# One block of a two-block network on one core: another interleaving of the state-space branch with its projections

## The chip, the cores and the metric

One core of a Trainium2 chip runs the whole program. The metric is the device time of one execution in microseconds (us), the median of several runs.

## The reference, cut to what matters

The network has two blocks. The first mixes tokens in two branches (a neighbourhood attention, "na", and a bidirectional state-space branch, "SSD") and then runs a mixture of 16 experts; the second block is a transformer of two layers. The change lies in the SSD branch and at its seam with the attention. There are 512 tokens and 256 context tokens, 4 groups of 8 heads of 64, chunks of 128 tokens (4 chunks, and 2 of context) and a state of 128. All of it is float32.

```python
xbc = silu(dwconv(h @ w_in[xBC], conv_w, conv_b))        # width 5, along the tokens
xs, Bm, Cm = split(xbc)
dt = softplus(dt_raw + dt_bias); a = dt * A; a_cs = cumsum(a) in a chunk
states = einsum(Bc, exp(a_cs[-1] - a_cs), x)              # one per chunk and direction
h = decay * h + states                                    # scan over the chunks
y_diag = (C B^T * exp(a_cs[l] - a_cs[s])) @ x             # inside a chunk
y_off  = (C @ h_prev) * exp(a_cs)
y = y_f + y_b + d_skip * xs
u = y * silu(z); u = u * rsqrt(mean(u*u over a group) + eps) * g   # z = h @ w_in[z]
```

## The kernel before, in words

Each engine has a program of its own, written as Python generators; a step ends at `yield`. Semaphores order the engines. `weave(main, filler, per)` and `pace(main, filler, plan)` merge two generators on each engine: `weave` puts one filler step in whenever `per` has added up to 1, `pace` puts plan[i] filler steps ahead of main step i. So PE, ScalarE (act), VectorE (dve) and GpSimd (pool) each execute the merged order strictly.

**Main: `pe_chunks(g)` and its fellows**, 15 steps a group. Five *state steps*, here S0 to S4: in each, VectorE or GpSimd weighs x by decay (`weigh`, L1028), PE makes two state products (L1039), VectorE adds them to the carried state (L1206 to L1215). In S0 to S3 the previous group's output is scaled to unit mean square (`dve_scale_z`, `pool_scale_z`, after `act_rstd`), turned by PE (`pe_finish`) and stored (`act_finish`). Then ten *chunk steps*, C0 to C9; n counts half chunks of four heads. ScalarE makes the exponents of half chunk n+1 (eight one-head passes, L1124, from rows that `load_rows` fetches by DMA, L1104) and the exponential of half chunk n (L1133); VectorE selects (L1252); GpSimd multiplies by C B^T (L1306, the matrix M of a half chunk); two steps later PE multiplies M by x (`pe_second`, L1072) and at odd n adds the products with the states (L1079). GpSimd and VectorE sum the parts (L1268, L1316 to L1320, L1277), VectorE multiplies by silu(z) (L1280), and ScalarE squares the result (`act_second`, L1167).

**Filler: `pe_proj(g+1)`**, 8 steps. Four convolution steps of x: PE products (L720, 10.5 us a step), two ScalarE copies into a padded row (L730, L733), five VectorE passes (L754, L758), two ScalarE silus (L739, L742), and PE turns the result of the step before (`pe_turn_x`). Then four z steps: one tile of z's products (L295, 7 us) and a silu by ScalarE (L956). `proj(0)` runs ahead of group 0, woven with `pe_dt` (the step sizes dt and their sums).

With per = 0.56 the filler steps of group g+1 fall behind the main steps S1, S3, C0, C2, C3, C5, C7 and C9: two convolutions in the state steps, two in the chunk steps, z in the rest. Beside group 3 run the attention's q and k products (`pe_na_qk` 0 and 1, L1531 and L1724, eight steps, the last two after the last main step). After that the attention (`pe_att_2`) has V's products (`pe_na_v`) as filler, by `PLAN1`; V reads a reordered copy of the input (`HTn`), made by `act_by_blocks` and `dve_by_blocks` in the room of B and C once `PHASE_C` (all of the SSD branch stored) is reached.

PSUM has 8 banks. Main takes from `PA` (five), the filler from `PG` (three), each time the bank that was taken longest ago, after a wait until it is free.

Of the kernel before, what the change touches and what calls it, by code (L numbers as in the profile page):

```python
# [157 lines left out]
def pace(main, filler, plan):  # L158

    for n in plan:  # L160
        for _ in range(n):
            next(filler, None)
        next(main, None)
    for rest in (main, filler):
        for _ in rest:
            pass

# [11 lines left out]
def build(nc, A, out):  # L179
    ctx = ExitStack()  # L180
    with ctx:
# [66 lines left out]
        PALL, PA, PG = list(range(8)), [3, 4, 5, 6, 7], [0, 1, 2]  # L248
        rings = [PS]
# [476 lines left out]
        def act_conv(act, nm, i, ti, dx, dc, before):  # L726
# [7 lines left out]
                *up(S("act_pad"), ("free", (nm, i, 2)), ("pad", (nm, i))))  # L734
            act.wait_ge(*at("acc", (nm, i)))
# [196 lines left out]
        def act_turn_x(act, g, i):  # L932
            key = ("tx", g, i, 4)
            act.wait_ge(*at("full", key))
            act.activation(xs2[g % 2][:, 4:6, i * 128:(i + 1) * 128], r3(PS.of(key)[:, 0:256], 128), ACT.Copy, bias=0.0, scale=1.0).then_inc(  # L935
                *up(S("act_xs"), ("free", key), ("xs", g, i, 4)))

        def act_proj(act, g):
            for i in range(4):
# [4 lines left out]
                act_conv(act, ("x", g), i, 4 * g + i, xsF[i % 2][:, 0:512], xsF[i % 2][:, 512:768], before)  # L944
                if g > 1 and i == 1:
                    act.wait_ge(*at("gone", g - 2, "pool"))
                    act.wait_ge(*at("gone", g - 2, "pe"))
                if i:
                    act_turn_x(act, g, i - 1)
# [81 lines left out]
        def pe_chunks(pe, g, pool):  # L1031
            xsT, BT = xs2[g % 2], BT2[g % 2]
            for m, (d, n, c) in enumerate(SWEEP):
# [6 lines left out]
                if d:  # L1040
                    if n in (2, 3) and g:
                        pe_finish(pe, g - 1, n - 2, pool)
# [67 lines left out]
        def act_exponents(act, g, n):  # L1110
# [7 lines left out]
            for d in range(2):  # L1118
# [16 lines left out]
        def act_chunks(act, g):  # L1135
            for d in range(2):
                load_rows(act, g, 0, d)
            for n in range(5):
                if n == 0 and g:
                    act_rstd(act, ("ssd", g - 1), ssy, 4)  # L1140
                if n in (2, 3) and g:
                    act_finish(act, g - 1, n - 2)
# [12 lines left out]
            if g == 3:  # L1155
                yield from idle(2)
                act_rstd(act, ("ssd", g), ssy, 4)
# [12 lines left out]
        def act_finish(act, g, part):  # L1170
            for i in (2 * part, 2 * part + 1):
# [5 lines left out]
                act.wait_ge(*now(S("act_fin")))  # L1177
                act.dma_start(yD[:, t, :], yTb[t % 2]).then_inc(*up(S(f"y_out{t % 2}"), ("yD", t), by=16))

        def dve_scale_z(dve, g):  # L1180
            zs = zs2[g % 2]
            dve.wait_ge(*at("uu", g, 3))
            dve_rstd(dve, ("ssd", g), ssy, 4, mean=512.0)
            dve.wait_ge(*at("rstd", ("ssd", g)))
            for c in (0, 2):
                dve.tensor_scalar(zs[:, c, :], zs[:, c, :], ssy[:, c:c + 1], None, ALU.mult).then_inc(*up(S("dve_zn"), ("zn", g, c)))

        def pool_scale_z(pool, g):
            zs = zs2[g % 2]
            pool.wait_ge(*at("rstd", ("ssd", g)))  # L1190
            for c in (1, 3):
                pool.tensor_scalar(zs[:, c, :], zs[:, c, :], ssy[:, c:c + 1], None, ALU.mult).then_inc(*up(S("pool_zn"), ("zn", g, c)))

        def dve_chunks(dve, g):
            for m in range(3):
                weigh(dve, 0, g, m)
            for m, (d, n, c) in enumerate(SWEEP):
# [18 lines left out]
                if d:  # L1216
                    if n == 0 and g:
# [10 lines left out]
            mark(("gone", g, "dve"), S("dve_y"))  # L1228
            if g == 3:
                yield from idle(2)  # L1230
                dve_scale_z(dve, g)

# [21 lines left out]
        def dve_second(dve, g, n):  # L1254
            c, hq = divmod(n, 2)
            if hq == 0:
                return
            for d in range(2):
# [3 lines left out]
                if c or g:  # L1262
                    pg, pc = (g, c - 1) if c else (g - 1, 3)
                    dve.wait_ge(*at("u", pg, pc) if d == 0 else at("ty1", pg, pc))
# [3 lines left out]
                dve.tensor_tensor(r3(TY[d], 64), r3(PS.of(key), 64), ev_, ALU.mult).then_inc(*up(S("dve_y"), ("free", key), ("ty", g, c, d)))  # L1268

        def dve_join(dve, g, n):  # L1270
# [5 lines left out]
            dve.wait_ge(*at("yd", g, c, 1))  # L1276
            dve.tensor_tensor(TY[0], PS.of(("y", g, c)), TY[0], ALU.add).then_inc(*up(S("dve_y"), ("free", ("y", g, c))))  # L1277
            dve.wait_ge(*now(S("dve_y")))
            dve.wait_ge(*at("zs", g, c))
            dve.tensor_tensor(zs[:, c, :], zs[:, c, :], TY[0], ALU.mult).then_inc(*up(S("dve_y"), ("u", g, c)))  # L1280

        def pool_chunks(pool, g):
            for m in range(3):
                weigh(pool, 1, g, m)
            for m, (d, n, c) in enumerate(SWEEP):
                weigh(pool, 1, g, m + 3)
                if d:
                    if n == 0 and g:
# [9 lines left out]
            if g == 3:  # L1298
                yield from idle(2)
                pool_scale_z(pool, g)  # L1300

# [6 lines left out]
        def pool_second(pool, g, n):  # L1308
# [419 lines left out]
        def act_by_blocks(act):  # L1728

            for kt in range(1, 8, 2):  # L1730
# [3 lines left out]
        def dve_by_blocks(dve):  # L1734
            for kt in range(0, 8, 2):
# [28 lines left out]
        def act_na_qk(act, n):  # L1764
            if n == 0:
                wait_all(act, SET0)
                act.dma_start(dcon, dsrc).then_inc(*up(S("dcon_in"), ("dcon",), by=16))
# [9 lines left out]
        def act_na_v(act, m):  # L1777
            for i in range(6):
# [26 lines left out]
        def dve_na_v(dve, m):  # L1805
            for i in range(6):
# [81 lines left out]
        PLAN1 = [0, 2, 1, 1, 1, 1] + [1, 1, 1, 1, 2] + [1, 1, 1, 1, 0] + [1, 0, 1, 1, 0, 1] + [1, 1, 1, 1, 0] + [1, 2, 1, 2, 1, 2, 1, 2, 2, 2]  # L1888
# [839 lines left out]
        def chain(*parts):  # L2728
            for part in parts:
                yield from part  # L2730

# [203 lines left out]

        def sp_program(sp):
# [4 lines left out]
            for g in range(3):  # L2941
                weave(idle(15), sp_proj(sp, g + 1), 0.56)
# [190 lines left out]
```

## Time and profile before

| | us |
|---|---|
| median of 3 runs | 4037.88 (4037.07 to 4039.29) |
| the profiled execution, its own time | 4034.85 |
| its span, first to last instruction | 4032.9 |
| SSD groups 0 to 3, first state product to last product with the states | 303.9 to 765.7 |
| granted TensorE clock, mean of the span | 0.967 |

PE is busy for 91% of the span, VectorE 28%, ScalarE 19%, GpSimd 11%. A row of the timeline gives start, duration, engine, line, operation and count, and in brackets the idle time before it with what released it. A float32 matmul of 512 columns shows as two records. ACTq is ScalarE's DMA issue.

### The profile page before, as it was taken

To read this page: it belongs to the slowest core of one execution; us is meant where nothing else is said; L and a number is where in the kernel's file an instruction comes from. 1 tells how busy PE (TensorE), PEld (TensorE's weight loads), DVE (VectorE), ACT (ScalarE), POOL (GpSimd) and SP (SyncE) were. 2 spreads that over 40 slices of the span, in tenths; PEclk is the share of its full clock that TensorE was granted. 3 is DMA by queue.
4 is the path that set the end of the run, shared out by engine and by line. 5 is a ranking of instruction groups with operands and counts; after the bars stand their busy time and mean duration, and the time that the engine had idled before them with its cause. 6 is when DMAs were issued, how large, how long until landed. Compare 5 with 4: busy or idle time off the path is not lost.

```text
span 4032.9 us, 32976 instructions
## 1 busy us (share of the span) xinstructions
PE 3663.4 (91%) x12600; PEld 1762.2 (44%) x12600; DVE 1137.1 (28%) x2594; ACT 782.8 (19%) x1786; POOL 450.8 (11%) x405
## 2 busy tenths in 40 slices
PE   6898888899999888888888888899999999999999
PEld 3354444444444443333233334555444445554444
DVE  2335444434310220311101114443221134432211
ACT  2024344322310210000000003332110123221100
POOL 1001223412100000000000002100221011012210
PEclk8899898999999989999999998999999999999999
DMA  7322223211212569999999992102222120022220
GB/s 253 125 75 75 79 63 94 87 37 50 79 63 88 189 250 409 409 409 409 409 409 409 409 398 73 37 27 84 83 72 80 51 90 32 28 97 69 84 71 34
DMA packets 302153, 634.08 MB, mean 157 GB/s; under 512 B 32499, under 2 KB 145763, under 8 KB 301743
## 3 DMA queue, kind: packets, MB, share of 16 engines
q1 hardware_dynamic: 240480, 591.96, 39.1%
q10 hardware_dynamic: 61519, 40.02, 3.5%
q8 instruction: 102, 1.67, 0.2%
q14 instruction: 52, 0.43, 0.0%
HBM read 625.50 MB, written 10.24 MB: 158 GB/s over the span
## 4 chain that ended last, share of the span: by engine, by line
PE 53%; DMA 18%; DVE 3%; SPq 1%; ACT 1%; issue 1%; POOL 0%; DVEq 0%; ACTq 0%
PE psum L295 26%; DMA arena<-in_w_exp_up_dram 7%; DMA arena<-in_w_exp_gate_dram 7%; PE psum L1531 6%; DMA arena<-in_w_exp_down_dram 4%; PE psum L2799 4%; PE psum L2763 4%; PE psum L2304 4%; PE psum L1359 2%; PE psum L1387 1%; PE psum L2784 1%; PE psum L2253 1%; PE psum L1368 1%; SPq L264 1%; PE psum L2694 1%
## 5 line engine op out<-in xcount | busy, mean ns | idle before, releaser
L295 PE MATMUL psum<-arena 128*128 128x512 f32 (+1 forms) x3200 | 1309.8, 568 | 17.1 <-ACT arena L935 11.9
L295 PEld LDWEIGHTS psum<-arena 128*128 128x128 f32 x3200 | 612.4, 193 | 699.2 <-issue 660.3
L2304 PE MATMUL psum<-arena 128*64 128x512 f32 x3072 | 696.5, 598 | 148.8 <-DMA arena<-in_w_exp_up_dram 76.2
L2304 PEld LDWEIGHTS psum<-arena 128*64 128x64 f32 x3072 | 234.4, 137 | 592.1 <-issue 571.6
L1531 PE MATMUL psum<-arena 128*128 128x512 f32 x768 | 352.8, 614 | 0.0
L720 PE MATMUL psum<-arena 128*128 128x512 f32 (+1 forms) x768 | 274.5, 517 | 1.3 <-ACT arena L538 1.3
L1531 PEld LDWEIGHTS psum<-arena 128*128 128x128 f32 x768 | 147.5, 196 | 193.2 <-issue 192.4
L1465 DVE CUSTOM_DVE_ANT_0 arena<-psum,arena 128x512 f32<-128x512 f32 (+3 forms) x224 | 114.0, 546 | 384.5 <-PE psum L1359 376.3
L2842 POOL TENSOR_SCALAR arena<-arena 128x512 f32<-128x512 f32 x88 | 138.6, 1576 | 696.2 <-ACT arena L2821 696.2
L720 PEld LDWEIGHTS psum<-arena 128*128 128x128 f32 x768 | 152.5, 201 | 125.4 <-issue 114.7
L2848 DVE SCALAR_TENSOR_TENSOR arena<-arena 128x512 f32<-128x512 f32 x88 | 66.2, 752 | 426.6 <-POOL arena L2842 426.6
L1407 ACT ACTIVATE arena<-arena 128x512 f32<-128x512 f32 (+3 forms) x224 | 134.3, 601 | 134.3 <-DVE arena L1465 133.7
L2369 DVE TENSOR_TENSOR arena<-arena,psum 128x512 f32<-128x512 f32 x32 | 22.0, 689 | 462.0 <-PE psum L2304 462.0
L2799 PE MATMUL psum<-arena 128*128 128x512 f32 x352 | 152.0, 592 | 0.0
L2763 PE MATMUL psum<-arena 128*128 128x512 f32 x352 | 151.7, 592 | 0.0
L2821 ACT ACTIVATE arena<-psum 128x512 f32<-128x512 f32 x88 | 52.5, 597 | 509.7 <-PE psum L295 478.2
L1368 PE MATMUL psum<-arena 128*128 128x128 f32 x576 | 85.7, 277 | 55.9 <-DVE arena L1472 30.7
L1542 POOL TENSOR_TENSOR arena<-arena 128x512 f32<-128x512 f32 x48 | 61.3, 1277 | 608.3 <-ACT arena L1538 595.2
L307 PE MATMUL psum<-arena 128*128 128x128 f32 (+3 forms) x442 | 67.6, 300 | 53.4 <-ACT arena L730 18.9
L1368 PEld LDWEIGHTS psum<-arena 128*128 128x128 f32 x576 | 68.4, 142 | 107.6 <-DVE arena L1472 38.1
L2763 PEld LDWEIGHTS psum<-arena 128*128 128x128 f32 x352 | 66.6, 189 | 84.7 <-issue 84.7
L2206 POOL TENSOR_TENSOR arena<-arena 128x128 f32<-128x128 f32 x32 | 12.9, 433 | 809.1 <-PE psum L307 593.2
(276 smaller groups left out, 3022.9 us busy)
## 6 DMA issues: line engine op xcount, KB each, us to landing
arena<-in_w_exp_gate_dram SPq DMA_DIRECT2D x128, 1024.0 KB, 18.6
arena<-in_w_exp_up_dram SPq DMA_DIRECT2D x128, 1024.0 KB, 18.6
arena<-in_w_exp_down_dram SPq DMA_DIRECT2D x128, 1024.0 KB, 18.8
arena<-in_w_in_dram SPq DMA_DIRECT2D x64, 1024.0 KB, 5.3
arena<-in_w_up_dram SPq DMA_DIRECT2D x88, 512.0 KB, 4.8
arena<-in_w_ada_dram SPq DMA_DIRECT2D x24, 1024.0 KB, 7.9
arena<-in_w_down_dram SPq DMA_DIRECT2D x20, 1024.0 KB, 4.9
arena<-acs_scratch ACTq DMA_DIRECT2D x64, 256.0 KB, 4.5
```

The lines of the kernel that those rows point to most:

```text
L295: mm = pe.matmul(shaped(b, l, r), l, r, start=kt == 0, stop=kt == nkt - 1)
L307: t = pe.transpose(b[0:m, c * k:(c + 1) * k], x, ident[0:k, 0:k])
L720: mm = pe.matmul(b[:, 0:z - a], wt(nm, kt, 512)[:, i * 128:(i + 1) * 128], HT[:, kt, a:z], start=kt == 0, stop=kt == 7)
L1359: pe.matmul(b[:, 0:u.nk], J.queries(u, a, z), J.keys(u, a, z), start=True, stop=True).then_inc(*up(S("pe_score"), ("full", ("s2", J.id, i, ...
L1368: t = pe.transpose(b[:, 128 * j:128 * j + 128], J.score(i, c)[:, 128 * j:128 * j + 128], ident)
L1407: act.activation(J.score(i, c), J.score(i, c), ACT.Exp, bias=sv2(i, c)[:, 0:1], scale=-1.0, accum_out=sv2(i, c)[:, 1:2]).then_inc(*up(S("a ...
L1465: dve.tensor_tensor_reduce(out=J.score(i, c), in0=PS.of(("s2", J.id, i, c))[:, 0:u.nk], in1=J.table(u, c), scale=-J.scale(u), scalar=3.0e3 ...
L1531: mm = pe.matmul(b, wt(nm, kt, 256)[:, i * 128:(i + 1) * 128], src[:, kt, 0:512], start=kt == 0, stop=kt == 7)
L2304: mm = pe.matmul(banks[n][64 * j:64 * j + 64, :], lhs[:, kt, 64 * j:64 * j + 64], w, start=kt == 0, stop=kt == 2 * nkb - 1)
L2763: mm = pe.matmul(banks[i], actT[:, kt, i * 128:(i + 1) * 128], wt(nm, kt, 512), start=kt == 0, stop=kt == 21)
L2799: mm = pe.matmul(b, actT[:, kt, i * 128:(i + 1) * 128], wt(nm, kt, 512), start=kt == 0, stop=kt == 21)
L2842: pool.tensor_scalar(accs3[n % 4], pads3[n % 4][:, 0:512], w3(L, 0, ti_of(s, i)), None, ALU.mult).then_inc(*up(S("pool_acc"), ("acc3", L, n)))
```

## The change

It does seven things.

1. `pace` with `PLAN0` takes the place of the weaves. Each group now has z tiles 1 to 3 of its own group ahead of S0, S1 and S2; the four convolution steps of the next group ahead of C0, C2, C4 and C6; z tile 0 of the next group ahead of C8. So `proj(0)` runs only five steps ahead of group 0, woven with `dt`.
2. The eight q and k steps run ahead of C0, C1, C2, C4, C5, C6, C8, C9 of group 3, and V's first two tiles ahead of its last two (idle) steps. V's `HTn` copies now wait for the last product of group 3 alone. `PLAN1` gives no V tile between the first two attention steps.
3. Banks: main `PA1` = 4 to 7, filler `PG1` = 0 to 3.
4. The product inside a chunk is added to the state part at once by VectorE (`dve_second`), and GpSimd's two additions come in another order.
5. The scale of a group's output: ScalarE computes rsqrt straight from the sums (`act_z_guess`, one table set), in S1; VectorE scales three tiles and GpSimd one, in S2; the turns come in S3 and S4.
6. `load_rows` for n+1 is issued after all eight exponent passes of n, not after the first four.
7. `act_turn_x` stands between the pad copies and the silu. The load of `dcon` is issued earlier.

```diff
         PALL, PA, PG = list(range(8)), [3, 4, 5, 6, 7], [0, 1, 2]
+        PA1, PG1 = [4, 5, 6, 7], [0, 1, 2, 3]
...
-                if d == 0:
-                    for e in range(2):
-                        load_rows(act, g, n + 1, e)
+            for d in range(2):
+                load_rows(act, g, n + 1, d)
...
-                if n == 0 and g:
-                    act_rstd(act, ("ssd", g - 1), ssy, 4)
-                if n in (2, 3) and g:
-                    act_finish(act, g - 1, n - 2)
+                if n == 1 and g:
+                    act_z_guess(act, g - 1)
+                if n in (3, 4) and g:
+                    act_finish(act, g - 1, n - 3)
...
+        def act_z_guess(act, g):
+            act.preload_act_table_set(LNEXP)
+            act.wait_ge(*now(S("act_uu")))
+            act.wait_ge(*at("eps"))
+            act.activation(small[:, 0:4], ssy, ACT.Ln, bias=eps, scale=1.0 / 512).then_inc(*up(S("act_rs")))
+            act.wait_ge(*now(S("act_rs")))
+            act.activation(small[:, 0:4], small[:, 0:4], ACT.Exp, bias=0.0, scale=-0.5).then_inc(*up(S("act_rs"), ("rs", ("ssd", g))))
...
+            dve.wait_ge(*now(S("dve_y"), 1))
+            dve.tensor_tensor(TY[0], PS.of(("y", g, c)), TY[0], ALU.add).then_inc(*up(S("dve_y"), ("free", ("y", g, c)), ("tyy", g, c)))
...
-            pool.tensor_tensor(TY[0], TY[0], TY[1], ALU.add).then_inc(*up(S("pool_ty"), ("ty1", g, c)))
             pool.wait_ge(*now(S("pool_ty")))
-            pool.tensor_tensor(TY[0], TY[0], TY[2], ALU.add).then_inc(*up(S("pool_ty"), ("ty3", g, c)))
+            pool.tensor_tensor(TY[1], TY[1], TY[2], ALU.add).then_inc(*up(S("pool_ty")))
+            pool.wait_ge(*at("tyy", g, c))
+            pool.wait_ge(*now(S("pool_ty")))
+            pool.tensor_tensor(TY[0], TY[0], TY[1], ALU.add).then_inc(*up(S("pool_ty"), ("ty3", g, c)))
...
         def act_by_blocks(act):
+            act.wait_ge(*at("gone", 3, "pe"))
...
         def dve_na_v(dve, m):
+            if m == 0:
+                dve_na_rope(dve, 1, 3)
+                dve_by_blocks(dve)
+                dve.wait_ge(*at("gone", 3, "pool"))
...
-        PLAN1 = [0, 2, 1, 1, 1, 1] + [1, 1, 1, 1, 2] + [1, 1, 1, 1, 0] + [1, 0, 1, 1, 0, 1] + [1, 1, 1, 1, 0] + [1, 2, 1, 2, 1, 2, 1, 2, 2, 2]
+        PLAN1 = [0, 0, 1, 1, 1, 1] + [1, 1, 1, 1, 2] + [1, 1, 1, 1, 0] + [1, 0, 1, 1, 0, 1] + [1, 1, 1, 1, 0] + [1, 2, 1, 2, 1, 2, 1, 2, 2, 2]
...
+        PLAN0 = (([1, 1, 1, 0, 0] + [1, 0] * 5) * 3 + [1, 1, 1, 0, 0] + [1, 1, 1, 0, 1, 1, 1, 0, 1, 1] + [1, 1])
...
-            weave(pe_proj(pe, 0, PALL), pe_dt(pe), 0.5)
-            for g in range(3):
-                weave(pe_chunks(pe, g, PA), pe_proj(pe, g + 1, PG), 0.56)
-            main = pe_chunks(pe, 3, PA)
-            for _ in range(3):
-                next(main)
-            weave(main, chain(pe_na_qk(pe, 0, PG), pe_na_qk(pe, 1, PG)), 0.57)
+            banks = PALL[:]
+            proj = pe_proj(pe, 0, banks)
+            weave(take(proj, 5), pe_dt(pe), 0.5)
+            banks[:] = PG1
+            filler = chain(proj, *[pe_proj(pe, g, PG1) for g in (1, 2, 3)], pe_na_qk(pe, 0, PG1), pe_na_qk(pe, 1, PG1), pe_na_v(pe, 0, PG))
+            pace(chain(*[pe_chunks(pe, g, PA1) for g in range(4)]), filler, PLAN0, False)
```

The other engines' programs change in the same way.

## Rows read from the trace of the kernel before

**Rows 1.** Busy time by stretch: groups 1, 2, 3, then to the attention's first turn.

```profile
422.80:460.40 37.60, 33.62 (x107) 18.74 (x106) 19.83 (x32) 10.58 (x16) 6.99 (x5) 0.95 0.25 83
460.40:549.60 89.20, 75.67 (x241) 42.06 (x240) 41.62 (x65) 47.75 (x107) 27.35 (x22) 0.89 0.24 72
549.60:678.90 129.30, 111.61 (x347) 61.90 (x346) 61.80 (x97) 58.42 (x123) 34.33 (x27) 0.89 0.25 73
678.90:765.70 86.80, 77.79 (x254) 42.55 (x253) 49.34 (x96) 36.91 (x95) 37.73 (x29) 0.94 0.38 113
765.70:823.20 57.50, 47.91 (x136) 24.95 (x136) 17.46 (x44) 14.30 (x27) 13.93 (x19) 0.91 0.18 54
```

**Rows 2.** PE's waits, 270 to 800 us: total, times, longest.

```profile
PE psum L307 <- ACT arena L730: 18.9, 6, 5.7
PE psum L1072 <- POOL arena L1306: 12.1, 8, 2.8
PE psum L295 <- ACT arena L935: 11.9, 3, 4.0
```

**Rows 3.** Timeline of PE in group 1.

```profile
460.66 10.49 PE L720 MATMUL psum<-arena 128*128 128x512 f32 x32
...
512.38 1.94 PE L1079 MATMUL psum<-arena 128*128 128x512 f32 x4
514.16 7.04 PE L295 MATMUL psum<-arena 128*128 128x512 f32 x16
...
537.21 1.97 PE L1072 MATMUL psum<-arena 128*128 128x64 f32 x8 [2.76 <-POOL arena L1306]
538.97 3.73 PE L1079 MATMUL psum<-arena 128*128 128x512 f32 x4
```

**Rows 4.** Timeline of ScalarE in C0 to C3 of group 1.

```profile
483.43 0.49 ACT L742 ACTIVATE arena<-arena 128x256 f32<-128x256 f32 x1
...
485.39 0.93 ACTq L1104 DMA_DIRECT2D arena<-acs_scratch  x2
...
487.65 1.28 ACT L1133 ACT_TABLE_LOAD   x1
488.95 0.63 ACT L1133 ACTIVATE arena<-arena 128x512 f32<-128x512 f32 x1
489.48 1.26 ACT L1124 ACTIVATE arena<-arena 128x128 f32<-128x128 f32 x4
...
493.93 0.36 ACT L733 ACTIVATE arena<-psum 128x256 f32<-128x256 f32 x1
...
500.31 0.72 ACT L739 ACTIVATE arena<-arena 128x512 f32<-128x512 f32 x1 [4.71 <-DVE arena L758]
```

**Rows 5.** Timeline of VectorE in the same group, the convolution's four later passes.

```profile
460.05 4.20 DVE L758 SCALAR_TENSOR_TENSOR arena<-arena 128x772 f32<-128x772 f32 x4
...
495.42 4.86 DVE L758 SCALAR_TENSOR_TENSOR arena<-arena 128x772 f32<-128x772 f32 x4
```

**Rows 6.** Timeline of GpSimd in the same group, the last two matrices M.

```profile
531.10 1.27 POOL L1306 TENSOR_TENSOR arena<-arena 128x512 f32<-128x512 f32 x1 [7.90 <-ACT arena L1133]
...
535.89 1.27 POOL L1306 TENSOR_TENSOR arena<-arena 128x512 f32<-128x512 f32 x1
```

**Rows 7.** Timeline of PE ahead of group 0: z tiles 0 and 1, then dt's sums.

```profile
271.38 13.93 PE L295 MATMUL psum<-arena 128*128 128x512 f32 x32
...
286.36 0.57 PE L829 MATMUL psum<-arena 128*128 128x192 f32 x2 [0.40 <-DVE arena L882]
```

**Rows 8.** Timeline of all engines at the seam to the attention.

```profile
784.00 3.65 PE L307 MATMUL psum<-arena 128*128 128x128 f32 x16 [8.00 <-POOL arena L1192]
...
787.94 0.69 ACT L1176 ACTIVATE arena<-psum,arena 128x512 f32<-128x512 f32 x1 [0.97 <-DMA yT_scratch<-arena]
...
799.25 0.46 ACTq L1676 DMA_DIRECT2D arena<-rpb_copies  x1
...
807.49 0.69 DVE L1465 CUSTOM_DVE_ANT_0 arena<-psum,arena 128x512 f32<-128x512 f32 x1 [7.54 <-POOL arena L1694]
```

More of the change, by code:

```diff
@@ L155, in weave, with pace @@
         pass
-def pace(main, filler, plan):
+def pace(main, filler, plan, empty=True):
     for n in plan:
@@ L163, in pace, with chain, take @@
         next(main, None)
-    for rest in (main, filler):
+    for rest in (main, filler) if empty else (main,):
         for _ in rest:
             pass
+def chain(*parts):
+    for part in parts:
+        yield from part
+def take(steps, n):
+    for _ in range(n):
+        next(steps)
+        yield
 def run(steps):
@@ L724, in pe_conv, with act_conv @@
                 mm.then_inc(*up(S("pe_conv"), *keys))
-        def act_conv(act, nm, i, ti, dx, dc, before):
+        def act_conv(act, nm, i, ti, dx, dc, before, between=None):
             pad, prev = pads1.take((nm, i))
@@ L734, in act_conv @@
                 *up(S("act_pad"), ("free", (nm, i, 2)), ("pad", (nm, i))))
+            if between:
+                between()
             act.wait_ge(*at("acc", (nm, i)))
@@ L933, in act_turn_x @@
             key = ("tx", g, i, 4)
+            if g > 1 and i == 0:
+                act.wait_ge(*at("gone", g - 2, "pool"))
+                act.wait_ge(*at("gone", g - 2, "pe"))
             act.wait_ge(*at("full", key))
@@ L943, in act_proj @@
                     before = [("full", ("BF", 3, 2))]
[L944 to L949, printed above, removed]
+                act_conv(act, ("x", g), i, 4 * g + i, xsF[i % 2][:, 0:512], xsF[i % 2][:, 512:768], before,
+                         (lambda: act_turn_x(act, g, i - 1)) if i else None)
                 yield
@@ L1227, in dve_chunks @@
                 yield
-            mark(("gone", g, "dve"), S("dve_y"))
+            mark(("gone", g, "dve"), S("dve_u"))
             if g == 3:
-                yield from idle(2)
+                yield
                 dve_scale_z(dve, g)
+                yield
         def dve_first(dve, g, n):
@@ L1298, in pool_chunks @@
             if g == 3:
-                yield from idle(2)
+                yield
                 pool_scale_z(pool, g)
+                yield
         def pool_first(pool, g, n):
@@ L1734, in dve_by_blocks @@
         def dve_by_blocks(dve):
+            dve.wait_ge(*at("gone", 3, "pe"))
             for kt in range(0, 8, 2):
@@ L1777, in act_na_v @@
         def act_na_v(act, m):
+            if m == 0:
+                act_by_blocks(act)
+                act.wait_ge(*at("gone", 3, "pool"))
             for i in range(6):
@@ L2997, in act_program @@
             weave(act_bc(act), act_ada_rest(act), 1)
-            weave(act_proj(act, 0), act_dt(act), 0.5)
-            for g in range(3):
-                weave(act_chunks(act, g), act_proj(act, g + 1), 0.56)
-            main = act_chunks(act, 3)
-            for _ in range(3):
-                next(main)
-            weave(main, chain(act_na_qk(act, 0), act_na_qk(act, 1)), 0.57)
+            proj = act_proj(act, 0)
+            weave(take(proj, 5), act_dt(act), 0.5)
+            filler = chain(proj, *[act_proj(act, g) for g in (1, 2, 3)], act_na_qk(act, 0), act_na_qk(act, 1), act_na_v(act, 0))
+            pace(chain(*[act_chunks(act, g) for g in range(4)]), filler, PLAN0, False)
             wait_all(act, PHASE_C)
-            act_by_blocks(act)
             act.wait_ge(*at("rpb"))
@@ L3067, in pool_program @@
             pool_start(pool)
-            run(idle(8))
-            for g in range(3):
-                run(pool_chunks(pool, g))
-            main = pool_chunks(pool, 3)
-            for _ in range(3):
-                next(main)
-            weave(main, chain(pool_na_qk(pool, 0), pool_na_qk(pool, 1)), 0.57)
+            filler = chain(idle(27), pool_na_qk(pool, 0), pool_na_qk(pool, 1), idle(6))
+            pace(chain(*[pool_chunks(pool, g) for g in range(4)]), filler, PLAN0, False)
             pool_near_zero(pool)
@@ L3077, in pool_program @@
             pool_near_mid(pool, 0)
-            pace(pool_att_2(pool, NEAR), chain(idle(12), pool_na_qk(pool, 2), pool_na_qk(pool, 3), idle(20)), PLAN1)
+            pace(pool_att_2(pool, NEAR), chain(filler, idle(6), pool_na_qk(pool, 2), pool_na_qk(pool, 3), idle(20)), PLAN1)
             pool_branch_na(pool)
```

67 lines of the change are left out of this document (32 added, 35 removed).

## The prediction, as it was put on record

> **What bounds the kernel now.** I read the page first, then busy time by stretch, PE's waits, and the timelines of PE, ScalarE, VectorE and GpSimd. Everything behind the attention's start is work that the diff leaves alone, so it moves as a block; what counts is when PE gets there. Groups 1 and 2 take 126.8 and 129.3 us [rows 1]. PE's work in a group at full clock is 97.2: four convolution steps at 10.3 and four z tiles at 6.9 from start to start [rows 3], 8.6 of state products, 7.0 of M's products, 6.9 with the states, 5.9 of turns and small ones. So some 30 us a group are waits or slow clock. The waits end on a padded copy (18.9 us over the branch), on M (12.1) and on a turned copy (11.9) [rows 2]; the granted clock is 0.89 in the chunk steps [rows 1]. After a wait of only 2.8 us the eight M records and four state records take 5.5 us, where the latter four alone take 3.7 against 1.9 [rows 3]: half speed, 1.2 GHz for 2.4.
>
> What the reader should see next is whose chain the waits end. ScalarE is busy for 47.8 of 89.2 us in the chunk steps [rows 1], yet between two convolution silus it never rests: it works, issues DMAs, or waits for the five VectorE passes between padded copy and silu, in order. From one silu's end (483.8) to the next (501.3) are 17.5 us [rows 4], against 14.7 of PE's work in such a pair of steps (10.3 convolution, 0.65 turn, 3.7 products).
>
> **The change, part by part.**
>
> *Banks four and four.* The waits on L730 and L935 are for one of the filler's three banks: a convolution takes two, its turns two more. With four they go, 30.8 us in all [rows 2]. What is late next is the chain behind M.
>
> *Four convolutions beside the chunks.* Now each pair C(2j), C(2j+1) holds one on ScalarE. The loop from silu end to silu end, from [rows 4]: eight exponent passes 2.5; issue of rows 0.95; table load and exponential 1.8; then a wait, since the rows are asked for only after all eight passes: 4.1 from issue to use (485.39 to 489.48), of which 2.8 are filled, so 1.3; eight passes 2.5; issue 0.95; exponential 0.55; the square 0.75, and 0.3 of wait, as GpSimd needs 4.8 us between two M [rows 6]; padded copies 0.85; VectorE's five passes 0.65 + 4.2 [rows 5]; silus 1.05. That is 18.4, and PE's 14.7 is hidden under it. It holds three times a group, once without the square (17.4).
>
> The chunk steps then take: first convolution 10.3, padded copy 0.45, VectorE 4.85, silus 1.05, that is 16.7 to the first silu's end; 17.4 + 18.4 + 18.4 to the fourth, 70.9; from there passes 2.5, table and exponential 1.8, M 1.3, and the last M 4.8 + 1.3 after it [rows 6]: 82.6. PE has then waited some 5 us (M of the last half chunk is all that is left behind z tile 0) and does its last products at half speed, 5.5 us as in [rows 3]. Sum 88.1, where the chunk steps now take 89.2 [rows 1]. PE's work there is only 65.6, so 22 us stay idle or slow: at C2 and C3 6 us, at C5 and C7 up to 4 each, at C8/C9 8.
>
> *z beside the states.* Three z tiles 20.7, states 8.6, turns 2.4: 31.7 of work. New waits: x's last turn now stands right ahead of the first state product, which needs VectorE's copy and weighing (1.4 us of passes, 1.8 taken). In S3 the output's turns wait for the scaling: VectorE, after the state additions of S2 (1.9 behind PE), does five small operations (1.0) and three tiles, not two (2.0): less PE's 1.7 of products, 3.4. Behind it the states' additions are queued and two banks of main's four come late, 0.7; slow clock 1.4. Sum 39.0, now 37.6 in group 1. The shorter rsqrt chain (one table set for two) costs and gives nothing: it lies beside S1 and S2.
>
> A group thus takes 39.0 + 88.1 + 0.3 = 127.4 against 126.8 and 129.3, mean 128.05. For the three groups with convolutions, group 0 taken like the others: -2.
>
> *Ahead of group 0.* The sums over dt wait for a product that VectorE ends at 286.3. Now z tiles 0 and 1 cover that, and 0.40 remain [rows 7]. With tile 0 alone PE is through at 278.35: a wait of 8.0, less the 0.4. The sums and the turn behind it lose 1.4 in slow clock and in a copy that tiles 2 and 3 covered. Sum +9.
>
> *Group 3.* Now 86.8 [rows 1] with six q and k tiles. Without a convolution ScalarE's loop is 6.7 a half chunk (2.5 + 4.2 of rows), PE's 10.6: PE bound, chunk steps 83.6 of work and 1.4 slow. Two of the eight tiles (20.7) and z tiles 1 to 3 (20.7) with a turn (0.65) are work done earlier or later than now, so 39.0 + 85.0 - 42.0 = 82.0; I keep 1 for small waits: 83 for 86.8, -4.
>
> *The seam.* Now a wait of 8.0 for the scaling, at 776.0 [rows 8]. The new order puts V's first tiles there. They need the reordered input; on VectorE that stands behind the last chunk's sums (4.2 us after PE's last product), the last rope (2.4) and four copies (1.4): 8.0. So one wait of 8 takes the place of another. Then come the two tiles (14), which hide the scaling, and the turns. Behind the turns everything of the attention's first softmax is serial: ScalarE stores four tiles, each pair waiting for the store two before (787.94, issued 2.1 earlier), so storing ends 7.9 after the turns begin; tables are asked for at 8.3; from there to the first reduction is 8.2 (799.25 to 807.49) [rows 8]; four reductions, two exponentials and the weights, at 0.6 to 0.7 a pass, 5: 21.4. PE's cover is turns 1.8, scores 3.4 with their banks, and one V tile 7: 12.2. Before, a k tile (11) and two V tiles (14) stood here, and 1.6 remained. So +9.2 - 1.6 = +7.6, and 1.4 of slow clock: +9.
>
> *At nothing.* Adding the inner product at once moves a VectorE pass ahead of GpSimd's two; the chain of sums keeps its length less one pass (0.7), and that is under the ScalarE loop. The moved `dcon` load lies among stores of ScalarE (0.35 of issue). The SP queue has the same loads in the same order and the same slots, so it runs no earlier and no later. If its cover were gone, a 1 MB load is some 5 us.
>
> **The Trainium skill against the rows.** In the timeline the pass behind a table load starts 1.30 us after the load (487.65 to 488.95), and nothing lies ahead of it [rows 4]. The Trainium skill, "ScalarE: Activation LUTs", section "What ACT_TABLE_LOAD costs", has about 1.28 us for the load and 1.38 more for a drain at every switch. That would put 1.4 on each of the nine loops, some 12 us in all, and make it 4063; the row shows no drain, and the 17.5 us loop measured here closes without one.
>
> **Sum.** +9 (head) -2 (groups) -4 (group 3) +9 (seam) = +12. The profiled execution was 4034.85 us, 3.0 under the median of the runs; on the median 4037.9 + 12 = 4050.
>
> **Bounds.** Each loop lies between PE's own 14.7 and 20.3 (VectorE's passes as slow as beside GpSimd, 4.86 and 1.05 for the first, and every rows' wait at its longest); slow clock between none (-2.7 at each group's end, -1.4 at each S3) and all. I take the middle since the measured loop of 17.5 is the nearest row. The head's wait is certain to 1.5, the seam's to 3.
>
> **The rivals.**
>
> *A, faster: ScalarE's loop does not bind.* It speaks for it that the waits which ScalarE now suffers in rows 4 are partly late PE banks, and PE is then given work in larger pieces. If the loop were PE's 14.7, a group's chunk steps would shrink by 11, three groups by 33: 4017. It decides from a loop 2.2 us shorter than forecast (20 us over nine loops cover the 12 and the 8 of the bound), that is under 16.2. Against it: the in-order wait for five VectorE passes is in every loop. Chance 0.19.
>
> *B, no change: the clock holds.* If PE stays at 2.4 GHz over waits under 4 us, the last products of three groups give back 8, S3 and the seam 4: 4038. Against it stands the 2.8 us wait in rows 3. Chance 0.24.
>
> *C, slower still: the row loads.* Asked for later, they meet SP's 1 MB loads. If each second load of rows comes 1 us later, and VectorE's passes take 0.7 more as at 495.42 [rows 5], nine loops cost 15: 4065. Chance 0.20. The Trainium skill, "GPSIMD Engine Reference", section 1 "Specifications", says that GpSimd shares its SBUF interfaces with VectorE where that has two SBUF inputs; rows 5 agree (4.86 beside GpSimd, 4.20 alone), and in the new order GpSimd is idle in most of the convolutions, which is why I take 4.2.
>
> My forecast, 4050, has 0.37.
>
> **Range and chances.** A measurement of this kernel can tell about 0.2%, 8 us. Faster by more: 0.19 (A). Within: 0.24 (B). Slower: 0.57 (forecast and C); that side's own range is 4046 to 4066. For eight in ten I take 4018 to 4066: it leaves out a loop at or under PE's own 14.7 (0.08) and the upper part of C (0.1).
>
> **What would show it.** Right: PE waits for M (L1306's successor) grow from 12 us to some 45; the waits on L730 and L935 are gone; a wait near 7.5 us ahead of the dt sums; a wait near 8 for `HTn` and one near 9 ahead of the attention's first turn; the silu ends 18 to 19 us apart in the chunk steps, the groups 127 us apart; granted clock there not above 0.9. Wrong: silus under 16.2 us apart, or groups under 120; V's first tile without a wait; or an execution in which the two seam waits are there and the groups have still shrunk.

## The result, and the profile after

The kernel after takes 4053.76 us (median of 5 runs, 4049.4 to 4056.83), the kernel before beside it 4037.88: 1.0038 times as long, interval 1.0023 to 1.0052. A second series (e5_after, below) gave 1.0035. The profiled execution took 4051.11 us, with a span of 4049.2 against 4032.9, so 16.3 more.

Where they lie is read from busy time by stretch, with the columns of [rows 1]. The rows are a stretch of 87.7 us from the end of group 1's first convolution step to group 2's first state product (most of group 1's chunk steps), the chunk steps of group 3 from its second q and k tile on, the stretch from the last product with the states to the attention's first turn, and the first attention of the second block, whose code the diff leaves alone.

```profile
461.10:548.80 87.70, 73.07 (x251) 43.95 (x251) 42.81 (x68) 44.58 (x101) 25.84 (x21) 0.88 0.22 61
713.00:788.50 75.50, 75.50 (x260) 43.32 (x258) 38.14 (x77) 30.78 (x82) 34.30 (x26) 1.00 0.33 92
788.50:831.30 42.80, 27.31 (x74) 12.32 (x73) 12.09 (x33) 10.66 (x21) 9.78 (x15) 0.86 0.16 49
2506.20:2760.20 254.00, 231.40 (x845) 124.63 (x844) 114.10 (x404) 72.86 (x208) 30.63 (x26) 0.93 0.12 38
```

The same 845 records of the last row take 246.5 us in the profile before:

```profile
2497.50:2744.00 246.50, 223.38 (x845) 120.63 (x844) 113.92 (x404) 72.78 (x208) 30.67 (x26) 0.96 0.12 39
```

The attention's first turn (PE turns the first softmax weights, L1401; all of the branch and its seam lies ahead of it) comes at 831.28, where it came at 823.21: +8.1. At 1205 us the distance is still 8.0. So half of the 16.3 lies in the branch and its seam, and 7.5 in unchanged code at a lower granted clock (0.93 for 0.96). The second profile (e5_after) tells what that is worth.

PE's waits from 270 to 850 us (total, times, longest), beside those of [rows 2]:

```profile
PE psum L1085 <- POOL arena L1338: 44.3, 17, 4.1
PE psum L319 <- POOL arena L1222: 10.0, 3, 3.6
PE psum L307 <- DVE arena L1771: 7.9, 1, 7.9
PE psum L843 <- DVE arena L896: 7.7, 1, 7.7
PE psum L1401 <- DVE arena L1510: 7.1, 1, 7.1
```

The waits for the filler's banks (30.8 us) are gone. PE now waits for M (L1338) instead, 12.1 us grown to 44.3, and three single waits of 7 to 8 us stand at the head (L843) and the seam (L307, L1401). The output's turns in S3 wait three times for the scaling (L319, 10.0 in all), and the waits ahead of state products fell from 15.9 us (L1039 before) to 5.7 (L1052). Rows from one group in PE's timeline show the price of one M:

```profile
412.73 7.46 PE L307 MATMUL psum<-arena 128*128 128x512 f32 x16
...
446.34 1.06 PE L319 MATMUL psum<-arena 128*128 128x128 f32 x8 [3.20 <-POOL arena L1222]
...
451.69 10.49 PE L732 MATMUL psum<-arena 128*128 128x512 f32 x32
...
480.25 1.97 PE L1085 MATMUL psum<-arena 128*128 128x64 f32 x8 [3.45 <-POOL arena L1338]
482.01 3.54 PE L1092 MATMUL psum<-arena 128*128 128x512 f32 x4
...
496.36 1.00 PE L1085 MATMUL psum<-arena 128*128 128x64 f32 x8
...
534.33 1.97 PE L1085 MATMUL psum<-arena 128*128 128x64 f32 x8 [3.18 <-POOL arena L1338]
536.09 3.73 PE L1092 MATMUL psum<-arena 128*128 128x512 f32 x4
539.61 0.71 PE L307 MATMUL psum<-arena 128*128 128x512 f32 x1
```

Behind a wait of 3.45 us the eight records take 1.97 us, without one 1.00: half speed, so such a wait costs itself and, as an estimate from these rows, some 2.6 us more (1.0 here, 1.6 in the four records behind). From z tile 1 to z tile 1 (412.73 to 539.61) a group takes 126.9 us, its state steps 39.0 (to 451.69).

ScalarE's timeline in the same chunk steps, one loop from silu to silu:

```profile
485.51 0.49 ACT L756 ACTIVATE arena<-arena 128x256 f32<-128x256 f32 x1
...
489.32 1.28 ACT L1145 ACT_TABLE_LOAD   x1 [0.99 <-DVE arena L1283]
490.62 0.63 ACT L1145 ACTIVATE arena<-arena 128x512 f32<-128x512 f32 x1
492.04 1.28 ACT L1137 ACTIVATE arena<-arena 128x128 f32<-128x128 f32 x4 [0.79 <-DMA arena<-acs_scratch]
...
497.25 0.63 ACT L1179 ACTIVATE arena<-arena 128x512 f32<-128x512 f32 x1 [0.77 <-DVE arena L1311]
...
497.88 0.58 ACT L742 ACTIVATE arena<-psum 128x512 f32<-128x512 f32 x1
...
503.65 0.72 ACT L753 ACTIVATE arena<-arena 128x512 f32<-128x512 f32 x1 [3.35 <-DVE arena L772]
504.28 0.49 ACT L756 ACTIVATE arena<-arena 128x256 f32<-128x256 f32 x1
```

The loops of this group are 17.35, 18.78 and 18.77 us; those of group 0 are 17.76, 19.88 and 19.80. Between two silus ScalarE waits for rows (0.79), for u, VectorE's product with silu(z), ahead of the square (0.77) and for the convolution passes (3.35), strictly in that order.

### The profile page after: what moved, and what is told of

Its sections match the earlier page's. It is cut to its first block, busy times and chain, and to the rows that moved or that the text cites. A ratio compares the mean times of both kernels' runs of the same rounds, so it can differ in the third digit from the quotient of the medians.

```text
span 4049.2 us, 32990 instructions
## 1 busy us (share of the span) xinstructions
PE 3665.0 (91%) x12600; PEld 1763.4 (44%) x12600; DVE 1140.6 (28%) x2598; ACT 772.5 (19%) x1778; POOL 448.7 (11%) x401
## 4 chain that ended last, share of the span: by engine, by line
PE 51%; DMA 19%; DVE 3%; SPq 1%; ACT 1%; issue 1%; POOL 0%; DVEq 0%; ACTq 0%
PE psum L307 26%; DMA arena<-in_w_exp_up_dram 7%; DMA arena<-in_w_exp_gate_dram 7%; PE psum L1564 6%; DMA arena<-in_w_exp_down_dram 4%; PE psum L2836 4%; PE psum L2800 4%; PE psum L2345 3%; PE psum L1392 2%; PE psum L1420 1%; PE psum L2821 1%; PE psum L2294 1%; PE psum L1401 1%; SPq L276 1%; PE psum L2735 1%
## 5 line engine op out<-in xcount | busy, mean ns | idle before, releaser
L307 PE MATMUL psum<-arena 128*128 128x512 f32 (+1 forms) x3200 | 1306.0, 566 | 10.5 <-DVE arena L1771 7.9
L307 PEld LDWEIGHTS psum<-arena 128*128 128x128 f32 x3200 | 612.6, 193 | 689.4 <-issue 658.0
L1564 PEld LDWEIGHTS psum<-arena 128*128 128x128 f32 x768 | 145.3, 193 | 187.8 <-issue 187.0
L732 PEld LDWEIGHTS psum<-arena 128*128 128x128 f32 x768 | 150.2, 198 | 123.8 <-issue 112.9
L1401 PE MATMUL psum<-arena 128*128 128x128 f32 x576 | 87.1, 280 | 62.9 <-DVE arena L1505 30.2
L1401 PEld LDWEIGHTS psum<-arena 128*128 128x128 f32 x576 | 69.1, 143 | 114.7 <-issue 39.3
L1392 PE MATMUL psum<-arena 64*128 64x512 f32 (+6 forms) x448 | 105.2, 547 | 0.4 <-ACT arena L1188 0.4
L2800 PEld LDWEIGHTS psum<-arena 128*128 128x128 f32 x352 | 66.7, 190 | 84.6 <-issue 84.6
L2836 PEld LDWEIGHTS psum<-arena 128*128 128x128 f32 x352 | 66.5, 189 | 83.7 <-issue 83.7
```

Source lines behind the costliest of these rows:

```text
L307: mm = pe.matmul(shaped(b, l, r), l, r, start=kt == 0, stop=kt == nkt - 1)
L732: mm = pe.matmul(b[:, 0:z - a], wt(nm, kt, 512)[:, i * 128:(i + 1) * 128], HT[:, kt, a:z], start=kt == 0, stop=kt == 7)
L1392: pe.matmul(b[:, 0:u.nk], J.queries(u, a, z), J.keys(u, a, z), start=True, stop=True).then_inc(*up(S("pe_score"), ("full", ("s2", J.id, i, ...
L1401: t = pe.transpose(b[:, 128 * j:128 * j + 128], J.score(i, c)[:, 128 * j:128 * j + 128], ident)
L1564: mm = pe.matmul(b, wt(nm, kt, 256)[:, i * 128:(i + 1) * 128], src[:, kt, 0:512], start=kt == 0, stop=kt == 7)
L2800: mm = pe.matmul(banks[i], actT[:, kt, i * 128:(i + 1) * 128], wt(nm, kt, 512), start=kt == 0, stop=kt == 21)
```

## The experiments

Times are medians; "ratio" is to the kernel before on the same chip, with a 95% interval. "First turn" is that of the attention, 823.2 us before and 831.3 after.

**e1_thin: is ScalarE's loop the bound?** Of the five VectorE passes of each convolution of x, three are left out (three taps are missing).

```diff
-            for j in range(1, 5):
+            for j in ((4,) if nm[0] == "x" else range(1, 5)):
```

> The changed kernel with two of VectorE's five passes in each convolution of x (three taps are left out). My theory (ScalarE's in-order loop through the convolution binds the chunk steps): each silu-to-silu loop falls from 18.8 to about 15.6 us, a group from 126.5 to about 114, and the dt sums come 3 us sooner: some 40 us in all, 4013. Rival A (PE with its banks binds there, the loop does not): the groups keep 126 and only the 3 us ahead of group 0 go: 4050.

4010.42 us, ratio 0.9924 (0.9909 to 0.9939). The silus now come 14.5, 16.2 and 15.6 us apart, the groups 109.7, 115.4 and 114.0, and PE waits less for M:

```profile
PE psum L1085 <- POOL arena L1338: 18.8, 6, 3.9
...
PE psum L843 <- DVE arena L896: 4.5, 1, 4.5
```

The first turn comes at 795.9, 35 us earlier. ScalarE and VectorE are each busy for half of the 87.7 us shown for the kernel after (44.6 and 42.8), and yet three passes of 1.05 us off each loop moved PE: the loop over both is what it waits for. Rival A does not hold.

**e2_head: the head alone.** All eight steps of `proj(0)` ahead of group 0 again.

```diff
-            weave(take(proj, 5), pe_dt(pe), 0.5)
+            weave(proj, pe_dt(pe), 0.5)
...
```

> The changed kernel with all eight steps of proj(0) ahead of group 0, woven with dt, and no filler in the state steps of group 0. My theory: the 7.7 us wait ahead of the dt sums and 1.3 us of slow clock go, 4045. Rival: the first state product then waits for the same VectorE chain, nothing is won, 4054.

4045.16 us, ratio 1.0014 (1.0005 to 1.0024); the wait on L896 is gone, and the first turn comes at 828.7. That is 2.6 and 4.3 us earlier than in the two profiles of the kernel after, for a wait of 7.7: the loops of group 1 are 17.7, 19.8 and 19.8 us here, longer than in the first of them (e3 shows by what). The time is the expected one.

**e3_rows: the row loads asked for early again.**

```diff
-            for d in range(2):
-                load_rows(act, g, n + 1, d)
+                if d == 0:
+                    for e in range(2):
+                        load_rows(act, g, n + 1, e)
```

> The changed kernel with load_rows after the first four exponent passes again. My theory: the waits for rows (0.8 and 0.25 us each time) go, each loop falls from 18.8 to 17.8 us, a group by 3 to 4, three groups by 10: 4043. Rival: the second load then stands waiting for the selection two half chunks before, ScalarE loses what it wins, 4054.

4051.21 us, ratio 1.0032 (1.002 to 1.0044): nothing gained. My theory missed by 8 us, and the mechanism that the rival named was not at work either. In the chunk steps beside a convolution the waits for rows are gone; the square's wait has grown in their place. ScalarE, then VectorE, then GpSimd:

```profile
495.46 0.63 ACT L1180 ACTIVATE arena<-arena 128x512 f32<-128x512 f32 x1 [3.07 <-DVE arena L1312]
```

```profile
493.69 1.74 DVE L1312 TENSOR_TENSOR arena<-arena 128x512 f32<-128x512 f32 x1 [6.45 <-POOL arena L1355]
```

```profile
488.56 1.27 POOL L1339 TENSOR_TENSOR arena<-arena 128x512 f32<-128x512 f32 x1 [11.34 <-ACT arena L1146]
489.79 1.04 POOL L1349 TENSOR_TENSOR arena<-arena 128x512 f32<-128x512 f32 x1
490.98 1.27 POOL L1352 TENSOR_TENSOR arena<-arena 128x512 f32<-128x512 f32 x1
492.39 1.27 POOL L1355 TENSOR_TENSOR arena<-arena 128x512 f32<-128x512 f32 x1
493.62 1.27 POOL L1339 TENSOR_TENSOR arena<-arena 128x512 f32<-128x512 f32 x1
```

GpSimd makes M and the three sums in one row (488.56 to 493.66), u follows, and beside GpSimd's next M it takes 1.74 us where it takes 0.69 otherwise; then the square, and only behind it the padded copies. The loops of group 1 are 16.7, 20.0 and 19.9 us. So the chain of sums stands right behind ScalarE's loop: what ScalarE does earlier, it waits for longer.

These rows also explain why such loops come in two lengths, 18.8 and 19.8 us. In the kernel after, in the loops shown above, u began first and GpSimd's M was the one that stretched:

```profile
496.52 0.69 DVE L1311 TENSOR_TENSOR arena<-arena 128x512 f32<-128x512 f32 x1 [7.42 <-POOL arena L1354]
```

```profile
496.62 1.72 POOL L1338 TENSOR_TENSOR arena<-arena 128x512 f32<-128x512 f32 x1
```

Which of the two begins first is a matter of 0.1 us and changes between executions of the same kernel. Of the six loops that hold a square, two had the long u in the kernel after (both in group 0), three in its second profile, five in e2_head and all six in e3_rows. At 1.05 us each, four more of them are 4.2 of the 8 us by which e3 missed, and three more about 3 of what e2's first turn did not gain.

**e4_seam: the seam alone.** The last k tile runs behind group 3's last main step, the scaling right behind the sums, the reordered copies (`HTn`) behind the scaling, and `PLAN1` is as before.

```diff
...
             if g == 3:
-                yield
                 dve_scale_z(dve, g)
+                yield
+                dve_by_blocks(dve)
                 yield
...
-        PLAN0 = (([1, 1, 1, 0, 0] + [1, 0] * 5) * 3 + [1, 1, 1, 0, 0] + [1, 1, 1, 0, 1, 1, 1, 0, 1, 1] + [1, 1])
+        PLAN0 = (([1, 1, 1, 0, 0] + [1, 0] * 5) * 3 + [1, 1, 1, 0, 0] + [1, 1, 1, 0, 1, 1, 1, 0, 1, 0] + [1, 0])
...
```

> The changed kernel with another seam: the last k tile of the attention stands behind group 3's last main work, the scale of group 3 follows its sums at once, then the reordering copies, and V's tiles all stand in the attention again (PLAN1 as before). My theory: the waits of 7.9 and 7.2 us and 3 us of slow clock at the seam go, 4037. Rival: the wait for the reordered input comes back behind ScalarE's k copies and the tables come later, 5 us at most are won: 4049.

4030.43 us, ratio 0.998 (0.9971 to 0.999), where 4037 was expected; again on another chip (e10_seam_again):

> The same kernel as in the run with the seam's order undone, a second time and on the same chip as its combination with the head. It should give 0.998 of the kernel before, 4030, with the first attention turn near 817 us. If it comes out at 0.999 or above, the gain of the first run was in how that run fell and not in the seam.

4030.14 us, 0.9984 (0.9976 to 0.9993), first turn at 819.3. The timeline of PE at e4_seam's seam has no gap but 0.60:

```profile
780.06 7.03 PE L1568 MATMUL psum<-arena 128*128 128x512 f32 x16
786.92 3.62 PE L1761 MATMUL psum<-arena 128*128 128x256 f32 x16
791.14 1.94 PE L319 MATMUL psum<-arena 128*128 128x128 f32 x16 [0.60 <-POOL arena L1225]
...
794.80 14.03 PE L307 MATMUL psum<-arena 128*128 128x512 f32 x32
...
816.80 1.04 PE L1405 MATMUL psum<-arena 128*128 128x128 f32 x8
```

The k tile covers the scaling, the two V tiles cover storing, copies and softmax. The first turn comes at 816.8, 14.5 us earlier than in the kernel after (12.0 in e10), for two waits of 15.1 in all, and 6.4 earlier (4.0 in e10) than in the kernel before, whose wait of 8.0 [rows 8] is gone too.

**e5_after: the kernel after again**, for its spread.

> The changed kernel again, beside the other three. Its profile of before showed 8.1 us lost up to the attention's first turn and 7.6 more in the first attention of the second block, whose code is the same (254.1 against 246.5 us). My theory: the second part is no effect of the change but of where the slow clock falls, so it differs from execution to execution: the stage shows another length in a new profile, and the median comes out between 4046 and 4054. Rival: the change does that too (254 again, 4054).

4050.23 us, 1.0035 (1.0023 to 1.0046). Its first turn stands at 832.9, and its second attention takes 246.5 us, as before:

```profile
2507.50:2754.00 246.50, 223.39 (x845) 120.54 (x844) 113.90 (x404) 72.74 (x208) 30.63 (x26) 0.96 0.12 39
```

Its span is 4042.9 us, 10.0 over that of before, and 9.7 of them lie ahead of the attention. So the 7.5 us in unchanged code are no fixed cost of the change: this execution of the same kernel does not have them, and the stretch took between 246.5 and 251.4 us in the twelve other profiles, whichever kernel they were of.

**e6_late8: does a start that is 8 us late cost more than 8?** The kernel before, with nine matmuls more behind the first block's attention, ahead of the first product with `w_branch_na`.

> The kernel before with nine more matmuls of 512 columns (7.8 us of PE work, their result overwritten) ahead of the first product with w_branch_na. If time only adds up: 4045. If later stages change length with the moment at which they begin: the second block's first attention is off 246.5 us by up to 8, and the total off 4045 by as much, either way.

4044.41 us, 1.0022 (1.0012 to 1.0032): 7.8 us over 4036.62 for 7.8 us of matmuls. A delay costs itself in the median, within the 5 to 13 us of the interval. In its profile the second block's first attention took 251.4 us, 4.9 more than in that of before.

**e7_place: the filler's places as before, with banks four and four.** Two convolutions in the state steps, two in the chunk steps, and the full head.

```diff
-        PLAN0 = (([1, 1, 1, 0, 0] + [1, 0] * 5) * 3 + [1, 1, 1, 0, 0] + [1, 1, 1, 0, 1, 1, 1, 0, 1, 1] + [1, 1])
+        PLAN0 = ([0, 0, 1, 0, 1] + [0, 1, 0, 1, 1, 0, 1, 0, 1, 0] + ([1, 0, 1, 0, 1] + [0, 1, 0, 1, 1, 0, 1, 0, 1, 0]) * 2 + [1, 0, 0, 0, 0] + [1, 1, 1, 0, 1, 1, 1, 0, 1, 1] + [1, 1])
...
```

> The changed kernel with the filler steps where they were (convolutions ahead of S2, S4, C1 and C3, z from C4 on), all of proj(0) ahead of group 0, and everything else of the change kept (banks four and four, scaling in S2, sums at once). My theory: with two convolutions out of the chunk steps ScalarE's loop binds only twice a group, the waits on L730 and L935 stay away: a group takes some 118 us, the wait ahead of group 0 is gone, 4020. Rival: the chain behind M takes it all again, groups of 126, 4044.

4051.09 us, 1.003 (1.0018 to 1.0042): a miss of 31 us, and the rival's 4044 is too low as well. PE's waits:

```profile
PE psum L1085 <- POOL arena L1338: 33.2, 9, 6.9
PE psum L319 <- POOL arena L1222: 22.6, 3, 8.7
PE psum L1066 <- DVE arena L1245: 8.4, 2, 4.2
```

VectorE's timeline says why: the scaling of the output (L1217, in S2 of the new order) stands behind a convolution's passes, and in the next step the state additions stand behind another's.

```profile
439.38 2.08 DVE L772 SCALAR_TENSOR_TENSOR arena<-arena 128x772 f32<-128x772 f32 x2
...
445.99 1.71 DVE L1217 TENSOR_SCALAR arena<-arena 128x512 f32<-128x512 f32 x3
...
464.15 4.20 DVE L772 SCALAR_TENSOR_TENSOR arena<-arena 128x772 f32<-128x772 f32 x4
468.27 0.68 DVE L1242 TENSOR_TENSOR arena<-arena 128x512 f32<-128x512 f32 x1
```

So the new scaling does not suit the old places: the waits for M fell by 11 us against the kernel after, and those on L319 and L1066 took that back. The new places with the old scaling were not run.

**e8_banks: the kernel before with banks four and four alone.**

```diff
+        PA1, PG1 = [4, 5, 6, 7], [0, 1, 2, 3]
...
-                weave(pe_chunks(pe, g, PA), pe_proj(pe, g + 1, PG), 0.56)
+                weave(pe_chunks(pe, g, PA1), pe_proj(pe, g + 1, PG1), 0.56)
...
```

> The kernel before with the banks four and four in the SSD branch and nothing else. My theory: the waits on L730 and L935 (30.8 us) go and the waits for M grow by half of that, 4027. Rival: main, which holds the bank of a chunk's inner product until GpSimd's sums are done, now waits for banks itself, 4042.

4036.6 us, 1.0001 (0.9992 to 1.001): nothing gained where 10 us were expected, and the rival had the mechanism. The 30.8 us of waits for the filler's banks are gone and have become these:

```profile
PE psum L1073 <- POOL arena L1307: 25.8, 8, 6.4
PE psum L1073 <- DVE arena L1278: 19.9, 7, 4.6
PE psum L1040 <- DVE arena L1216: 9.7, 2, 4.8
```

M was next in line (12.1 before), and main, with one bank less, now waits for the one that holds the product inside a chunk (L1278 frees it). The third line was 7.9 before. The change's own edit 4 frees that bank early, so it has no such wait.

**e9_seamhead: seam and head together.**

> The kernel after, with the two undone parts that helped by themselves put together: all eight steps of group 0's projection ahead of group 0, and at the seam the last k tile behind the last main step of group 3, the scaling right behind the sums, the reordered copies behind the last softmax input is free, and no V tile before the attention. If the head's wait and the seam's waits are two separate costs, the first attention turn comes at about 813 us (the seam alone gave 816.8, the head alone 4.3 earlier than the kernel after) and the time is about 4026, 0.997 of the kernel before. Rival: both were bought from the same slack, so that it stays at the seam's 4030 or above.

4023.34 us, 0.9965 (0.9952 to 0.9979), first turn at 808.4 (4026 and 813 were expected). Two separate costs: on one chip 6.8 us under the seam alone.

**e13_late_join: the chain of sums out of the loop.** e9's kernel, with u (VectorE) and its square (ScalarE) one main step later, behind the next convolution.

```diff
-                if n >= 2:
-                    dve_join(dve, g, n - 2)
+                if n in (4, 6, 8, 9):
+                    dve_join(dve, g, 2 * (n // 2) - 3 if n < 9 else 7)
...
```

> The kernel with the seam and the head undone, and in the chunk steps VectorE's last multiplication of a chunk (u) and ScalarE's square of it one main step later, behind the next convolution instead of ahead of its padded copies (the last chunk as before). If the chain of sums stands right behind ScalarE's loop, the loops that hold a square lose their 0.6 to 0.8 us of wait for u and come to 18.0 us from 18.8, six of them with convolutions: 4019 from 4023, too little to be sure of. Rival: the time lost is in GpSimd's own order (three passes of sums ahead of M), then the loops shrink and PE's waits for M stay at 43 us and the time with them.

4014.47 us, 0.9943 (0.993 to 0.9955); 8.9 under e9's 4023.34 (same chip), where 4 was expected. The loops of group 1 are 18.1, 17.6 and 17.9 us, where e9's are 18.1, 19.8 and 18.8: 3.1 less in a group. The waits for M fall too, 43.0 to 37.2, so the rival does not hold. Part of the surplus is the long u: two of e9's six loops had it (one is the 19.8); here u no longer begins together with GpSimd's M, and none of the six has it.

**e14_join_rows: the same with early row loads**, the edit that gained nothing in e3.

> The same, and the rows asked for after four of the eight passes, as in the kernel before. Alone that edit gained nothing because the square then waited 3.1 us for u. With u and the square out of the way the loops should come to about 16.8 us, nine of them 1.2 to 2.0 shorter than now: 4010, and PE's waits for M near 30 us. Rival: GpSimd's sums or VectorE's convolution passes are next in line and the loop stays above 18: 4020.

4009.32 us, 0.993 (0.9916 to 0.9943). The median is the forecast one, but the intervals of e13 and e14 overlap, so a gain over e13 is not shown. The first turn comes at 793.5 for 800.7, and 3.7 of these 7.2 us lie ahead of group 0, where the two kernels have the same code. The loops of group 1 are 17.0, 17.7 and 17.7 us, not 16.8 throughout, and PE waits 34.3 us for M, where 30 were expected. So the 4010 came partly by luck, and the rival is right on what is next, though not with its 18 us, as VectorE's timeline shows:

```profile
474.87 0.75 DVE L1288 COPY_PREDICATED arena<-arena 128x512 f32<-128x512 int32 x1 [1.55 <-ACT arena L1137]
481.74 0.69 DVE L978 COPY arena<-psum 128x512 f32<-128x512 f32 x1 [6.12 <-PE psum L319]
482.35 1.33 DVE L768 TENSOR_SCALAR arena<-arena 128x772 f32<-128x772 f32 x1
483.72 4.20 DVE L772 SCALAR_TENSOR_TENSOR arena<-arena 128x772 f32<-128x772 f32 x4
```

The convolution's first pass now stands behind the copy of x's last turn, which waits for PE's turn, that is for PE's own convolution. This kernel is 0.7% faster than the one before and 1.1% faster than the one after.

## Why the prediction was right, and where it was not

The prediction was +12 us at the branch and 4050. The branch gave +8.1 and +9.7 in two profiles, the medians +15.9 and +13.6. The direction and most of the mechanism were right; that the median came within 4 us was partly luck. By the first profile the terms are +9.3 (head), +0.7 (groups), -7.8 (group 3) and +5.9 (seam), 8.1 in all, for +9, -2, -4 and +9. The 4 us by which the branch stays under its 12 are more than made up by 4 to 8 us of the medians' difference that no term holds.

- **Head, +9.** The wait ahead of dt's sums was 7.67 (8.0 forecast). The first state product came at 299.36 with two z tiles fewer before it, where 303.9 less their 13.8 us is 290.1: +9.3. Right.
- **Loops and groups, -2, measured +0.7.** Forecast 17.4, 18.4, 18.4; measured 17.35, 18.78, 18.77 in group 1, and 17.76, 19.88, 19.80 in group 0, whose u was the long one twice. State steps 39.0 as forecast, groups 1 and 2 126.9 and 126.1 for 127.4, M-waits 44.3 for 45. The step that failed is "group 0 taken like the others": from its first state product to the next group's it took 122.9 us, where it took 118.9 before (303.9 to 422.8), so it lost 4.0 where 0.65 were to be won. e1 shows that the loop is the cause, since three passes off it shrank the groups by 11 to 13. Rival A falls: no loop of the chunk steps was under 17.3 us.
- **Group 3, -4, measured -7.8.** From z tile 1 (665.75) to the last product 122.8 us, where 125 were forecast (39.0 + 85.0 + 1). PE was busy for all of the stretch shown of the chunk steps, at clock 1.00; the slow clock that I had put there did not come. Another 1.8 is a slip of the sum: the wait ahead of the first state product stands in the 39.0 but not in the 86.8 of before that it is set against. (The 3.4 put for S3's wait is 3.2 by its own terms; measured were 3.2, 3.2 and 3.6.)
- **Seam, +9, measured +5.9.** Both waits are there, 7.9 for 8.0 and 7.15 for 9.2. The mis-sized term is the stretch from the request for the tables to the first reduction: 8.2 was taken from [rows 8], and it took 5.0 (821.62 to 826.59). The request was 1.6 later than forecast, so 21.4 us became 19.6.
- **Slow clock.** Right: 1.97 us for 1.00 behind eight of the nine waits for M of 3.2 to 4.1 us (behind the ninth, of 3.63, 1.10, and only the four records after it were slow), granted clock 0.88 in the first row above. Rival B falls. A wait of 0.76 us is followed by eight records in 1.10.
- **Rival C.** The later row loads show as waits of 0.2 to 0.9 us, once or twice a loop, in groups 0 and 1, and of 1.5 in group 2 (1.3 was forecast), and taking them back alone gains nothing (e3). The convolution's four passes kept their 4.20 us. Its other half came by a path that I did not name: u beside GpSimd's M, 1.05 us a time.
- **"At nothing": the chain of sums.** This step failed too. I put it "under the ScalarE loop"; it is in it. The square waits 0.77 and 0.64 for u in group 1 of the kernel after, 1.99 and 2.00 in group 0, 3.07 in e3, and with u and its square one step later groups 0 to 2 came out 3.6, 3.1 and 2.9 us shorter (e13 against e9, 105.1, 125.7 and 123.6 for 108.8, 128.8 and 126.5). That I forecast 0.3 of wait there kept the error in the sum small.
- **The table load.** 490.62 follows 489.32 by 1.30 us: no drain of 1.4 us at a switch, as in [rows 4]. The Trainium skill, "ScalarE: Activation LUTs", section "What ACT_TABLE_LOAD costs", has about 1.38 us of drain at every switch; the trace does not bear that out.

What stays open is the difference between the branch's 8 to 10 us and the medians' 14 to 16. e6 shows that a delay costs itself. The last 7 us of the first profile are unchanged code at a lower clock, and the same stretch ran both long and short in other kernels: from the first turn to the end, in code that no edit but e6's touches, the thirteen profiles other than e6's took 3204.6 to 3217.9 us (before 3209.7, after 3217.9 and 3210.0). With one profile for each series I cannot say whether it is chance: e3 and e7, whose seams are those of the kernel after, lie 3 and 8 us above their first turns as well, and the five runs with the seam undone at most 2.4, which points at the seam; but e1, with the seam of the kernel after, lies at 0.3.

## What to carry to other kernels

A stage in which ScalarE and VectorE are each busy for half of the time, and PE for 83%, can still be bound by one loop: follow one item from an engine's step to its own next such step, through every engine that it waits for in order, and compare that with PE's work for the same item. A freed wait moves to what is next in line (banks to M, rows to the square), so test an edit together with the one that takes the next link away (rows early gained nothing alone; behind the move of u it came with 5 us, which the intervals do not part from nothing). At a stage's end, hold back one piece of work without inputs from that stage (here one k tile) for each serial chain that PE would wait out.

## What the runs showed of the hardware

- The attention of the second block, with the same code and the same 845 records, took 246.5 to 254.1 us in different executions, at a granted clock of 0.96 and 0.93. A difference of under 8 us between two single profiles can be this alone.
- A VectorE pass of 512 columns with two operands in SBUF took 0.69 us alone and 1.74 us beside a GpSimd pass that began 0.07 us before it (e3). Where VectorE's pass began 0.10 us before GpSimd's, it kept its 0.69 and GpSimd's took 1.72 for 1.27 (the kernel after). The convolution's first pass took 0.62 alone and 1.33 beside GpSimd (e14).
